# A hybrid decoder step on one core: sums of squares taken from rows, sequence states as stationary tiles, and eight gate quarters moved into the small tile's steps

## The reference

```python
def _l2norm(x):
    return x * lax.rsqrt(jnp.sum(x * x, axis=-1, keepdims=True) + EPS)

def _gated_delta_chunk(S, q, k, v, g, beta):          # one chunk; S is the state, 128 x 128 for a head
    ...
    rhs = beta[..., None] * (v - eg[..., None] * jnp.einsum('bhid,bhde->bhie', k, S))
    u = lax.linalg.triangular_solve(a_mat, rhs, left_side=True, lower=True, unit_diagonal=True)
    qk = jnp.einsum('bhid,bhjd->bhij', q, k) * decay
    o = eg[..., None] * jnp.einsum('bhid,bhde->bhie', q, S) + jnp.einsum('bhij,bhje->bhie', qk, u)
    S_new = jnp.exp(gc[..., -1])[..., None, None] * S + jnp.einsum('bhjd,bhj,bhje->bhde', k, w_last, u)
    return S_new, o
...
    qb = _l2norm(heads(qb, DK)) * (DK ** -0.5)
    kb = _l2norm(heads(kb, DK))
```

## Time and profile before

| what | value |
|---|---|
| median of three runs | 3359.25 us (3356.04 to 3359.67) |
| the profiled execution, its own time | 3357.9 us |
| its span, first to last instruction | 3356.1 us |
| PE busy | 3282.4 us, 98% of the span |
| DVE, ACT, POOL busy | 59%, 45%, 12% |
| mean granted TensorE clock | 0.991 |

### The profile page before, as it was taken

The page is one execution under the profiler, slowest core; times in us unless marked ns, Lnnn a source line. Parts: engine busy times, 40 slices in busy tenths (PEclk is TensorE's granted clock), DMA queues, the critical chain, the costliest instruction groups (busy, mean ns, idle before and its releaser), DMA issues. The chain is left out here.

```text
span 3356.1 us, 59861 instructions
## 1 busy us (share of the span) xinstructions
PE 3282.4 (98%) x24010; PEld 2901.8 (86%) x24010; DVE 1974.2 (59%) x3714; ACT 1503.9 (45%) x3116; POOL 393.0 (12%) x369
## 2 busy tenths in 40 slices
PE   8999999999999999999999999999999999999998
PEld 7877889999998877898998877889998877789897
DVE  6644535543546654685666654587575755478484
ACT  5424443222235554464554644455454644446362
POOL 3211000432503110000003100000001211000000
PEclk9989999999999999999999999999999999999999
DMA  4211113655743111354553211345463211246463
GB/s 159 64 43 50 33 58 110 226 194 204 253 148 109 53 45 57 120 158 138 164 192 109 72 39 45 113 132 165 141 211 124 71 46 45 77 128 184 120 182 98
DMA packets 142818, 392.51 MB, mean 117 GB/s; under 512 B 18288, under 2 KB 20288, under 8 KB 139072
## 3 DMA queue, kind: packets, MB, share of 16 engines
q1 hardware_dynamic: 142544, 388.69, 36.3%
HBM read 353.95 MB, written 35.69 MB: 116 GB/s over the span
## 5 line engine op out<-in xcount | busy, mean ns | idle before, releaser
L616 DVE TENSOR_TENSOR wl<-raw,wh 128x512 fp32r<-128x512 f32 (+1 forms) x795 | 749.8, 951 | 595.2 <-ACT wh L609 591.5
L609 ACT CAST wh<-raw 128x512 fp32r<-128x512 f32 (+1 forms) x795 | 635.8, 808 | 461.8 <-PE bank L880 379.3
L880 PE MATMUL bank<-xnT,wh 128*128 128x512 f32 (+2 forms) x2432 | 719.3, 379 | 10.8 <-ACT gate L1627 8.2
L880 PE MATMUL bank<-hnT,wh 128*128 128x256 f32 (+2 forms) x3016 | 580.5, 290 | 3.4 <-ACT V L1907 3.4
L880 PEld LDWEIGHTS bank<-xnT,wh 128*128 128x128 f32 x2432 | 427.4, 191 | 82.5 <-issue 16.6
L880 PEld LDWEIGHTS bank<-hnT,wh 128*128 128x128 f32 x3016 | 473.6, 188 | 8.8 <-ACT V L1907 4.2
L880 PE MATMUL bank<-hid,wh 128*128 128x512 f32 (+1 forms) x1760 | 467.5, 353 | 0.0
L880 PE MATMUL bank<-xnT,wl 128*128 128x512 f32 (+2 forms) x1280 | 459.1, 363 | 0.0
L880 PE MATMUL bank<-hnT,wl 128*128 128x256 f32 (+2 forms) x1508 | 437.2, 290 | 0.0
L880 PE MATMUL bank<-Tm,wh 128*128 128x256 f32 x2016 | 368.7, 282 | 0.6 <-ACT sg L1907 0.6
L880 PEld LDWEIGHTS bank<-hid,wh 128*128 128x128 f32 x1760 | 309.5, 188 | 45.8
(11 more groups left out here) (365 smaller groups left out, 4703.7 us busy)
## 6 DMA issues: line engine op xcount, KB each, us to landing
raw<-in_wstream SPq DMA_DIRECT2D x346, 512.0 KB, 3.5
raw<-wsum SPq DMA_DIRECT2D x252, 256.0 KB, 3.4
raw<-in_wstream SPq DMA_DIRECT2D x189, 256.0 KB, 2.7
ops_in<-in_wstream SPq DMA_DIRECT2D x44, 512.0 KB, 7.3
wsum<-ops_out SPq DMA_DIRECT2D x22, 1024.0 KB, 6.4
hT<-in_xT SPq DMA_DIRECT2D x4, 2048.0 KB, 9.0
out_yp_out<-hT SPq DMA_DIRECT2D x16, 512.0 KB, 2.9
xr<-in_x_prompt SPq DMA_DIRECT2D x12, 512.0 KB, 7.4
```

The costliest lines, as they stand in the source:

```text
L609: act.copy(hi_cell(n), raw_cell(n)).then_inc(sem("hi_done"), 1)
L616: nc.vector.tensor_tensor(lo_cell(n), raw_cell(n), hi_cell(n).bitcast(F32), ALU.subtract).then_inc(sem("lo_done"), 1)
L880: ins = nc.tensor.matmul(*a, **k)
```

## The change

**Sums of squares.** The `sqc` squares and the matmuls with ones are kept only for the first tile that a group works on (tile 0, and `"S"` in group 0): two of the five tiles in group 0, one of four in the others. For tile t + 1 the sums are now made in the second chunk of tile t: ACT squares the turned rows of k and q from PSUM into `q4["kn"]` and `q4["qn"]` (`row_squares`), DVE sums each head's 128 columns (`row_sums_of`), POOL makes the power and the factors (`row_factors`), and DVE's `delta_rows(t + 1)` moves behind the update of the state.

**States as stationary tiles.** In the small tile, the state `Sb[:, b, x]` becomes the stationary tile, and the eight columns of one sequence (four of `WT`, four of `qe`) the moving one: 32 matmuls in place of 64. ACT copies the result into `SWQ`; four transposes and four products with the identity bring it into the banks that held it before. The zeroed copies and 16 DVE copies go.

**Gate quarters.** `QUARTERS_0` loses its last two quarters (step 17) on each of four tiles; the small tile gets eight more: two around the new state products, and six in front of six of the nine steps of the state update (`S_FILL`). Attention steps of tile 0 shift: in the small tile `transposes` and `values` later, in the other groups' convolution `inputs` and the first `scores` one block earlier. SP asks for gate units 6 and 7 before it waits for the small tile's states.

```diff
-QUARTERS_S = (1, 1, 1, 1, 1, 1, 0, 0, 0, 0, 0, 0, 0, 2, 0, 0, 0, 0)
-QUARTERS_0 = (1, 1, 1, 0, 1, 1, 1, 1, 0, 1, 1, 0, 1, 0, 1, 0, 0, 2)
+QUARTERS_S = (1, 1, 1, 1, 1, 1, 0, 0, 1, 0, 0, 0, 0, 1, 2, 6, 0, 0)
+QUARTERS_0 = (1, 1, 1, 0, 1, 1, 1, 1, 0, 1, 1, 0, 1, 0, 1, 0, 0, 0)
+S_FILL = (0, 3, 4, 6, 7, 8)
-IN_DELTA_S = dict(inputs=1, scores=(2, 6), exp=(3, 7), transposes=(4, 8), values=(5, 13))
+IN_DELTA_S = dict(inputs=1, scores=(2, 6), exp=(3, 7), transposes=(5, 13), values=(6, 14))
-IN_CONV = dict(inputs=4, scores=(5, 7), exp=(5, 7), transposes=(6, 8), values=(7, 9))
+IN_CONV = dict(inputs=3, scores=(4, 7), exp=(4, 7), transposes=(6, 8), values=(7, 9))
+        heads_of = [(P, slice(1, 2))] + ([(NS, slice(0, 1))] if first else [])
+        head = slice(0 if first else NS, NS + P)
@@ SP
+                weights("gate", 7)
                 sp.wait_ge(*made("S_done", NH))
@@ PE, convolution
-                    for t in tiles:
+                    for t in tiles[:1 + F]:
@@ PE, small tile
+                    for x in range(NH):
+                        pair = WQ[:, x, 0:2 * CH].rearrange("p (s c) -> p s c", c=CH)
+                        out = bank[3][:, 2 * CH * x:2 * CH * (x + 1)].rearrange("p (s c) -> p s c", c=CH)
+                        for b in range(NB):
+                            own = slice(NMETA + NL * b, NMETA + NL * (b + 1))
+                            last = nc.tensor.matmul(out[:, :, own], Sb[:, b, x, :], pair[:, :, own], start=True, stop=True)
+                        if x == 1:
+                            gate_quarter()
+                    last.then_inc(sem("WS_ps"), 1)
+                    gate_quarter()
+                    attention_step(0, IN_DELTA_S, 14)
                     for x in range(NH):
-                        for b in range(NB):
-                            last = nc.tensor.matmul(bank[1][0:NS, P * x:P * (x + 1)], WTm[:, x, b, :], Sb[:, b, x, :],
-                                                    start=b == 0, stop=b == NB - 1)
+                        last = nc.tensor.transpose(bank[1][0:NS, P * x:P * (x + 1)], SWQ[:, x, 0, :], c("ident"))
                     last.then_inc(sem("WS_ps"), 1)
+                    delta_rows(0)
                     for x in range(NH):
-                        for b in range(NB):
-                            nc.tensor.matmul(bank[5][0:NS, P * x:P * (x + 1)], qeTm[:, x, b, :], Sb[:, b, x, :],
-                                             start=b == 0, stop=False)
+                        nc.tensor.matmul(bank[5][0:NS, P * x:P * (x + 1)], SWQ[:, x, 1, :], c("ident"), start=True, stop=False)
...
-                    delta_rows(0)
                     for b in range(NB + 1):
+                        if b in S_FILL:
+                            beside(t, 15, 1)
@@ ACT
-                        act.activation(sqc[:, live], post[:, j - 1, live], ACT.Square).then_inc(sem("sqc_done"), 1)
+                        act.activation(sqc[:, head], post[:, j - 1, head], ACT.Square).then_inc(sem("sqc_done"), 1)
+            def row_squares(t):
+                for q, (x, b) in enumerate((("kn", 6), ("qn", 2))):
+                    act.wait_ge(*made("nat_ps", 3 * ix[t] + q + 1))
+                    act.activation(q4[x][:].rearrange("p h e -> p (h e)"), bank[b][:], ACT.Square).then_inc(sem("sqc_done"), 1)
                 beside(t, 15)
+                if t != "S" and t + 1 < NT:
+                    row_squares(t + 1)
@@ POOL
+            def row_factors(t):
+                s, tt = t + 1, nc.gpsimd.tensor_tensor
+                f = lambda x: fac[:, s, x, :]
+                pool.wait_ge(*made("sums_in", 1 + F + 2 * t))
+                link(nc.gpsimd.tensor_scalar(rs8[:, s, :], rs8[:, s, :], EPS, None, ALU.add))
+                tt(rs8[:, s, :], rs8[:, s, :], nhalf[:, 0:2 * NH], ALU.pow).then_inc(sem("rs_done"), 1)
+                pool.wait_ge(*made("rs_done", F + 2 * t))
+                link(nc.gpsimd.tensor_scalar(f(0), rs8[:, s, 0:NH], P ** -0.5, None, ALU.mult))
+                tt(f(1), f(0), eg[:, s, 0:NH], ALU.mult)
+                tt(f(3), rs8[:, s, NH:], eg[:, s, NH:], ALU.mult)
+                link(tt(f(2), rs8[:, s, NH:], eg[:, s, 0:NH], ALU.mult))
+                tt(f(2), f(2), beta[:, s, :], ALU.mult).then_inc(sem("rs_done"), 1)
@@ DVE
-                scaled(t, ("kn", "qn", "qe"))
+                if t == "S" or t == 0:
+                    scaled(t, ("kn", "qn", "qe"))
+                    return
+                dve.wait_ge(*made("rs_done", F + 2 * t))
+                scaled(t, ("kn",))
+                dve.wait_ge(*made("rs_done", 1 + F + 2 * t))
+                scaled(t, ("qn", "qe"))
+            def row_sums_of(t):
+                for q, x in enumerate(("kn", "qn")):
+                    dve.wait_ge(*made("sqc_done", 2 * NH + 2 * t - 1 + q))
+                    v_.tensor_reduce(out=rs8[:, t + 1, NH * (1 - q):NH * (2 - q)], in_=q4[x][:], op=ALU.add, axis=AX.X).then_inc(sem("sums_in"), 1)
                         if k == 1 and t + 1 < NT:
-                            delta_rows(t + 1)
+                            row_sums_of(t + 1)
...
                         dve.wait_ge(*made("S_done", NH * (F + e + 1)))
+                        if k == 1 and t + 1 < NT:
+                            delta_rows(t + 1)
```

More of the change, by code:

```diff
@@ L1115, in attention_step, with beside @@
                         att_scores(t, gk)
-            def beside(t, k):
-                for _ in range(quarters_of(t)[k]):
+            def beside(t, k, quarters=None):
+                for _ in range(quarters_of(t)[k] if quarters is None else quarters):
                     gate_quarter()
-                if after(t) is not None:
+                if after(t) is not None and quarters is None:
                     attention_step(after(t), IN_DELTA_S if t == "S" else IN_DELTA, k)
@@ L1800, in delta @@
                 beside(t, 13)
+                if t == "S":
+                    act.wait_ge(*made("WS_ps", 1))
+                    turned_ps = bank[3][:].rearrange("p (h s c) -> p h s c", h=NH, c=CH)
+                    act.copy(SWQ[:, :, :, NMETA:], turned_ps[:, :, :, NMETA:NS]).then_inc(sem("small_done"), 1)
                 beside(t, 14)
@@ L2360, in beside @@
                         gate_small(quarters[0] // 4 - 1)
-                if after(t) is not None:
+                if after(t) is not None and parts is None:
                     attention_step(after(t), IN_DELTA_S if t == "S" else IN_DELTA, k)
@@ L2372, in delta @@
                 i, n, s, w = ix[t], n_of(t), slot(t), own_w(t)
-                if t in ("S", 0) and first or t and not first:
+                if t == "S" or t and not first:
                     delta_args(t)
@@ L2405, in delta @@
                     beside(t, 4 + 2 * q)
-                small = lambda b: slice(NMETA + NL * b, NMETA + NL * (b + 1))
-                if t == "S":
-                    step(v_.memset(WTm[:], 0.0))
-                    step(v_.memset(qeTm[:], 0.0))
-                    settle()
-                    dve.wait_ge(*made("bt_rd", 3))
-                    for b in range(NB):
-                        step(v_.tensor_copy(qeTm[:, :, b, small(b)], WQ[:, :, CH + small(b).start:CH + small(b).stop]))
-                    settle()
                 beside(t, 13)
```

75 lines of the change are left out of this document (43 added, 32 removed).

## The result

The changed kernel has a median of 3337.39 us over four runs (3335.03 to 3346.67), beside 3359.03 for the kernel before: ratio 0.9942, interval 0.9922 to 0.9963. It is faster by 0.6%, 22 us, where 28 were forecast; 3337 lies in the range and 6 us above the predicted 3331. Executions of this one kernel differ by more than the miss: nine of them, timed in two lots, go from 3335.03 to 3346.67 us, at mean clocks of 0.993 to 0.988. The profiled execution is the slowest of the four, with its own time of 3346.67 us; a second profile of the same program, taken later, has 3338.13. Where the two differ, both are named.

The account below looks back on a forecast made before the run. PE was taken as the bound, busy 98% of the span. Terms of -20.0, -6.2, -5.0, -6.0, +6.3 and +3.5 sum to -27.4 from 3357.9 us, 3330.5, stated as 3331; range of 8 in 10: 3314 to 3347.

Parts of the forecast that it names:

- likeliest case: Whole kernel: the forecast of 3331 us itself, chance 0.60, with its own range of 3322 to 3340.
- a small tile that still runs at 0.8: Sign of being wrong: the small tile's clock staying at 0.8 where near 0.9 was expected.
- sums of squares: Convolution windows: 96 of 136 sums leave PE at 0.232 us each, less small losses; -20.0 us.
- state products, at the full clock: Small tile: 32 products plus transposes and identity products replace 64, 16.7 us becoming 10.5; -6.2 us.
- waits in the small tile: Small tile: most of PE's 7.4 us of waits close through moved steps, dropped copies and cover; -5.0 us.
- waits in the tiles of group 0: Group 0's tile changes: new waits of 9.4 us replace old ones of 3.1, as quarters leave; +6.3 us.
- clock, small tile and tiles: Closed gaps give back -6.0 us of lower clock in the small tile; group 0's tile changes lose +3.5.
- The prediction's estimate from the Trainium skill: State products: from loading cost and gaps, 5.5 us won in the products where the rows make it 7.6.
- The chain before `kn`: Group 0's tile changes: squares, sums, power and scaling make PE wait 1.9 us three times, 5.7 us; hidden in other groups.
- 0.7 for bank 4 and most of the 3.0 for `X`: Group 0: new waits of 0.7 us for bank 4 at the first change, 1.95 in tile 1 and 1.05 in tile 3.
- The rival of POOL's power deciding every change: All tile changes: the 8-column power takes 5.81 us, making the kernel slower at 3363 us; chance 0.04.
- the three places on which it rested: Lower clock said to stand behind PE waits of 3.11 and 1.14 us in the small tile, and 0.97 at a tile change.

Follow-up runs that it names:

- wide_states: Changed kernel with its 32 state products given 64 to 8 moving columns in place of 8: 3335.71 us, in a second timing 3339.06 us.
- second_power: Changed kernel plus a useless 32-column power on POOL ahead of each tile's real one: 3401.57 us, ratio 1.013.
- row_sums_only: Kernel before with only the sums of squares changed; state products, quarters and attention steps as before: 3352.83 us, ratio 0.9979.
- one_quarter_back: Changed kernel with one gate quarter put back before each group 0 tile change, two instead of six among the small tile's updates: 3350.06 us, ratio 0.998.
- the wide ones: Changed kernel with 64 to 8 moving columns in state products, alone or with gate quarters moved too: medians 3335.06 to 3349.22 us.
- wide_cover_11: Changed kernel with 64 to 8 moving columns in state products and one quarter per group 0 tile moved from step 7 to 17: 3335.06 us.
- exp_values: Changed kernel with group 0's second exponentials at step 9 and the small tile's first product with values at step 7: 3336.32 us, ratio 0.9932.

## Why the prediction was right, and where its sum was off

The forecast and its likeliest case held: faster, by the sums and the state products, with new waits in group 0 alone. But one of its own signs of being wrong came: a small tile that still runs at 0.8. It was forecast near 0.9 and ran at 0.80 and 0.85, before at 0.82. And the convolution of group 1 became 4 us shorter, not 5.5, with PE at 83.91 of 86 us, 97.6%. That the median lies as near as 6 us is in part luck, as the terms show. Term by term, in us against the kernel before. PE's time from start to start was added up between matched places of the program, apart for the two levels of its clock.

| term | forecast | profiled execution | second profile |
|---|---|---|---|
| sums of squares | -20.0 | -19.6 | -20.0 |
| state products, at the full clock | -6.2 | -5.7 | -5.7 |
| waits in the small tile | -5.0 | -4.1 | -4.2 |
| waits in the tiles of group 0 | +6.3 | +6.8 | +6.8 |
| clock, small tile and tiles | -2.5 | +7.4 | +0.6 |
| clock behind the tiles (a stretch at 541 us) | 0 | +1.5 | +1.5 |

The clock's line is the time at the lower level, 52.0 us and 36.6 against 35.3 before, at the 45% that the prediction worked out for it. The terms make 13.7 and 21.0 us, the two executions were 11.2 and 19.8 under the 3357.9 of before. Of the remainders of 2.5 and 1.2 us about 1.1 lies behind group 3's tiles, up to the program's end (452.6 and 452.5 us from its first `oT` product on, before 451.5).

**Sums.** Right in its sum, and for a reason partly wrong. Group 0's convolution became 7.6 us shorter, not 4.2: the wait of 4.07 that DVE ends did not grow by what PE saved ahead of it, it shrank to 3.66, since DVE is itself fed by PE there. A part is chance: a stretch of 3.4 us at the lower clock at 120 us is not there in this execution. The other groups won 4.0 each, not 5.3, because two blocks now wait for ACT's square, 0.99 and 0.72 us, where one waited 0.66. As the prediction had it, PE stays the bound.

**State products.** The rows' price of 0.232 for the new form was 0.218 at the full clock. The price of 0.235 for the old form was too high for half of it: 0.235 is what a block of eight took with its change to `u`, while in the unbroken run of line 1322 (before) the records start 0.109 us apart from 216.32 to 221.45 us at the full clock, 0.218 a product.

```profile
216.30:221.40 5.10, 5.10 (x49) 5.10 (x48) 0.00 (x0) 0.00 (x0) 0.00 (x0) 1.00 0.01 3
```

That is the missing half us of this term. So a product cost the same in both forms, and what the change won is that there are 32 of them in place of 64. In `wide_states`, with up to 64 moving columns, 16 products took the same 3.49 us from start to start.

The prediction's estimate from the Trainium skill (TensorE: Matmul & The Clock Gate, section LDWEIGHTS) was 0.192 for the old form and 0.213 for the new, and the new one lies near the 0.218 by an omission: it counts the gap of the moving columns for the old form and not for the new. With the 25 ns that the Trainium skill's table of gaps has for up to 64 columns, the estimate for the new form would be 0.263. No difference between the forms is in the trace, so the measurement decides.

**The chain before `kn`.** It came out almost to the step: two reductions at 0.69 each (taken as 0.69), the power at 1.66 (taken as 1.70; the trace of before also has one of 1.70 on 4 columns, `hr`, so that the price follows the columns was a choice among its rows), the four handovers, for which the prediction named no row, at 0.06 to 0.13 (0.1), and a wait of 1.90 three times (1.9). The change from tile 0 to tile 1, up to the 301.85 of `d_kn` on PE:

```profile
298.22 0.68 DVE L2276 TENSOR_REDUCE rs<-d_qn 128x4 f32<-128x512 f32 x1
298.99 0.24 POOL L2026 TENSOR_SCALAR rs<-rs 128x8 f32<-128x8 f32 x1 [25.36 <-DVE rs L2276]
299.31 1.66 POOL L2027 TENSOR_TENSOR rs<-rs,nhalf 128x8 f32<-128x8 f32 x1
301.10 0.69 DVE L2256 TENSOR_TENSOR d_kn<-bank,rs 128x512 f32<-128x512 f32 x1 [0.56 <-POOL rs L2027]
```

Beside it 0.46 for `qn` at each change was not in the sum, nor the 2.17 for `sc`, which ACT finished late because its gate logits now stand ahead of the exponentials; and 0.7 for bank 4 and most of the 3.0 for `X` did not come (0.60 remained in tile 1). These happen to cancel, so the +6.3 is right by luck in its small terms and by its working in the 5.7. The rival of POOL's power deciding every change was excluded for the right reason, and `second_power` shows that it would have been the slower case had the price been there.

**The clock is the step that failed.** The prediction said: "The lower level follows PE's gaps", and "With those gaps closed I give a little over half back". The gaps were closed, 7.4 us of waiting to 3.3, and the lower level stayed: 38 us of it in the small tile of the profiled execution (95 x 0.20 x 2), 27 in the second, 30 before. One of the three places on which it rested was misread: before the change the level fell at 209.4 us, 2.5 us before the wait of 1.14 began that ends at 213.00, so not behind it. Behind the 3.11 and the 0.97 it does stand. After the change it came with PE fully busy, behind no wait (the first row is from before, the second from after):

```profile
209.40:216.10 6.70, 5.57 (x27) 5.18 (x27) 1.04 (x9) 0.00 (x0) 2.03 (x2) 0.50 0.00 0
...
200.50:217.50 17.00, 17.00 (x74) 15.98 (x73) 1.54 (x3) 0.37 (x1) 0.00 (x0) 0.50 0.00 1
```

That term, -2.5 in the sum, is +0.6 and +7.4 in the traces. With the stretch behind the tiles it makes 4.6 of the 7.6 us by which the second profile's own time missed the sum, and 11.4 of the 16.2 of the profiled execution.

**The move of the quarters** was costed for the cover it takes away, and that was right. Its other side was seen only as 0.7 us: with the sums made from rows, a fourth quarter in front of a change waits 3.8 us for bank 4. `row_sums_only` and `one_quarter_back` show it. The changed kernel has no quarter in front of a change, and its own fourth one, the 32nd, comes only behind the turned `kn` and `qn`.

## What to carry to other kernels

When work is put in front of a hand-over as cover, look at every bank that it writes, not only at the time that it fills: the same quarter covers a wait of 1.9 us or causes one of 3.8 by whether its small products need a bank whose reader has just been made later. A saving on the bound engine (20 us here) holds only where the replacement's chain doesn't end in that engine's next step; price the chain instruction by instruction from rows of the same number of columns. Closing waits is no way to count on a higher clock: the kernel with the fewest waits among the wide ones was the slowest of them. And a difference of 5 to 10 us that rests on the clock of a stretch with small matmuls needs several profiles of the same program: one can show 1.00 and the next 0.75.

## What the runs showed of the hardware

The granted clock of one stretch of the same program differed between executions, 1.00 and 0.75 over the small tile, which took 78 and 102 us with nearly the same waits (3.2 and 4.0 us). The lower level held for 44.4 us while PE was busy 99% of them. What starts it is open in part. At the tile changes it came with waits: with all nine waits of 3.03 us and all three of 7.41 in `second_power`, and with the three of 3.8 in `one_quarter_back`. In the small tile a stretch of 17 us began 12 to 16 us behind the last wait in the profiles of the changed kernel, `wide_cover_11` and `exp_values`, each time in the quarter between the two halves of the state products, and in that of `wide_states` none did; the moving columns of the state products did not decide it.

An f32 product, two records, took 0.218 us from start to start at the full clock with 48 stationary and 128 moving columns as with 128 stationary and 8 or up to 64 moving ones. And POOL's power grows with the columns, though not by them alone: on 128 rows 1.03 us for 4, 1.66 for 8 and 5.45 for 32, but 1.70 for another group of 4 (`hr`) and 2.06 for another of 8 (`rs` of the first tile).
